# A hybrid decoder block in float32 on one core: the output projection takes one 2x2 block problem in column groups 1 and 2, and the turns come directly behind the settling

## What is computed

```
    x = x + 0.5 * swiglu(rms_norm(x, ffn1_norm[l]), ffn1_w_gate[l], ffn1_w_up[l], ffn1_w_down[l])
    ...
    x = x + jnp.concatenate([y_conv, y_attn], axis=-1) @ w_out[l]
    x = x + 0.5 * swiglu(rms_norm(x, ffn2_norm[l]), ffn2_w_gate[l], ffn2_w_up[l], ffn2_w_down[l])
```

## Time and profile before

| | us |
|---|---|
| median of 3 runs | 1764.33 (1763.83 to 1764.43) |
| profiled execution, its own time | 1764.07 |
| its span, first to last instruction | 1762.2 |
| PE busy | 1750.1 (99%) |
| DVE busy | 1508.9 (86%) |
| ACT busy | 1052.0 (60%) |
| output projection, four groups | 977.5 to 1065.5 |

### The profile page before, as it was taken

The page is one execution under the profiler, slowest core; times in us unless marked ns, Lnnn a source line. Parts: engine busy times, 40 slices in busy tenths (PEclk is TensorE's granted clock), DMA queues, the critical chain, the costliest instruction groups (busy, mean ns, idle before and its releaser), DMA issues.

```text
span 1762.2 us, 21424 instructions
## 1 busy us (share of the span) xinstructions
PE 1750.1 (99%) x7797; PEld 1440.9 (82%) x7797; DVE 1508.9 (86%) x1741; ACT 1052.0 (60%) x1258; POOL 303.7 (17%) x585
## 2 busy tenths in 40 slices
PE   9999999999999999999999999999999999999998
PEld 7888888888888888888888888888888888888886
DVE  7799999999887786777877768899999999887786
ACT  7566666666555554555555456566666666555544
POOL 0102211111112112111121141021111111210001
PEclk9999999999999999999999999999999999999999
DMA  7756666666676667657555577666666666676654
GB/s 266 239 197 219 206 213 222 227 221 212 207 238 215 216 194 235 203 172 222 192 179 173 194 227 254 220 209 205 217 222 229 225 216 216 208 254 205 220 188 132
DMA packets 201801, 374.91 MB, mean 213 GB/s; under 512 B 19808, under 2 KB 20448, under 8 KB 201696
## 3 DMA queue, kind: packets, MB, share of 16 engines
q1 hardware_dynamic: 182848, 351.84, 60.6%
q0 software_dynamic: 18272, 21.01, 4.1%
q10 hardware_dynamic: 576, 0.69, 0.1%
HBM read 351.44 MB, written 4.19 MB: 202 GB/s over the span
## 4 chain that ended last, share of the span: by engine, by line
PE 98%; DVE 1%; DMA 1%; ACT 0%; issue 0%; SPq 0%; DVEq 0%; ACTq 0%
PE bank L854 17%; PE bank L856 17%; PE bank L857 17%; PE bank L871 9%; PE bank L873 9%; PE bank L872 9%; PE bank L992 4%; PE bank L995 4%; PE bank L994 4%; PE bank L837 2%; PE bank L836 2%; PE bank L835 2%; DMA raw<-in_ffn_w_gate_dram 0%; PE bank L1154 0%; PE bank L1171 0%; DMA x<-in_x_dram 0%
## 5 line engine op out<-in xcount | busy, mean ns | idle before, releaser
L1688 DVE TENSOR_TENSOR w_lo<-raw,w_hi 128x1024 fp32r<-128x1024 f32 x447 | 545.8, 1225 | 146.6 <-ACT w_hi L1249 142.2
L1249 ACT ACTIVATE w_hi<-raw 128x1024 fp32r<-128x1024 f32 x447 | 471.6, 1058 | 318.8 <-PE bank L857 195.8
L2478 POOL DMA_DIRECT2D turn_in<-gate x448 | 219.0, 497 | 820.2 <-DVE gate L1788 744.7
L854 PE MATMUL bank<-w_hi,xT_hi 128*128 128x512 f32 x812 | 318.3, 392 | 0.4 <-DVE xT_lo L1781 0.3
L856 PE MATMUL bank<-w_lo,xT_hi 128*128 128x512 f32 x812 | 316.0, 389 | 0.0
L857 PE MATMUL bank<-w_hi,xT_lo 128*128 128x512 f32 x812 | 316.0, 389 | 0.0
L854 PE MATMUL bank<-w_hi,hT_hi 128*128 128x512 f32 x528 | 205.5, 389 | 0.7 <-DVE w_lo L1688 0.7
L856 PE MATMUL bank<-w_lo,hT_hi 128*128 128x512 f32 x528 | 205.4, 389 | 0.0
L857 PE MATMUL bank<-w_hi,hT_lo 128*128 128x512 f32 x528 | 205.4, 389 | 0.0
L1263 ACT ACTIVATE w_hi<-first_b 128x1024 fp32r<-128x1024 f32 x140 | 148.7, 1062 | 91.0 <-PE bank L857 38.4
L1263 ACT ACTIVATE w_hi<-second_b 128x1024 fp32r<-128x1024 f32 x129 | 136.9, 1062 | 104.8 <-DVE second_b L1955 47.4
(11 more groups left out here) (239 smaller groups left out, 2865.0 us busy)
## 6 DMA issues: line engine op xcount, KB each, us to landing
raw<-in_ffn_w_down_dram SPq DMA_DIRECT2D x132, 512.0 KB, 4.9
raw<-in_ffn_w_up_dram SPq DMA_DIRECT2D x102, 512.0 KB, 6.4
raw<-in_ffn_w_gate_dram SPq DMA_DIRECT2D x101, 512.0 KB, 5.7
raw<-in_w_in_dram SPq DMA_DIRECT2D x80, 512.0 KB, 4.2
first_b<-in_ffn_w_gate_dram SPq DMA_DIRECT2D x40, 512.0 KB, 4.5
first_b<-in_ffn_w_up_dram SPq DMA_DIRECT2D x40, 512.0 KB, 4.6
second_b<-in_ffn_w_gate_dram SPq DMA_DIRECT2D x34, 512.0 KB, 5.2
second_b<-in_ffn_w_up_dram SPq DMA_DIRECT2D x34, 512.0 KB, 5.4
```

The lines of the kernel that those rows point to most:

```text
L854: pe.matmul(acc, hi[:, kt, ts], w_hi[slot][:, kk], start=(opens and kk == 0), stop=False, skip_group_check=problems(ffn, c) > 0)
L1249: act.activation(w_hi[f % RING][:], raw[m % RING][:], ACT.Copy).then_inc(hi_ready, 1)
L1688: dve.tensor_tensor(w_lo[f % RING][:], src[:], w_hi[f % RING][:].bitcast(F32), ALU.subtract)\
L2478: pool.dma_start(to[32 * j:32 * j + 32, q].rearrange("r k t i -> r (k t i)"), mid[32 * q:32 * q + 32, j].rearrange("r k t i -> r (k t i)") ...
```

## The change

The output projection gets one block problem: the first two K-chunks in order (`order[0]`, `order[1]`: the token tiles 8 to 11) of column groups 1 and 2. The two groups keep 6 plain chunks each, and the seven products stand among those of group 1. P1 and P6, P7 go to bank 5, P5 and P3 to bank 4, P2 and P4 straight onto the banks of group 1. Since the partial sums belong to two groups, DVE adds them onto `x` in six operations (`out_add`), after P1, P5, P6, chunk 4, P7 and P2; P3 waits for the second of these adds, P7 for the third, and the settling of groups 1 and 2 for all six. The sums of weight blocks are four operations in `low_out`. The token sums are made in the mixer's last part: `out_tokens` at B, chunk 4, `token_sum` at C, chunk 3, and the split at X, chunk 3 (ACT) and 5 (DVE). The weight blocks are read into `kept_down` and the buffers of parts K and V, four loads in place of four chunk loads.

Besides, `turn_quads` stands directly behind the settling of its group, ahead of the next split, and `split_block` moves: for block 0 to P7 of group 1, for block 1 to k = 4 of the 6 chunks of group 2, for block 2 as before to k = 6 of group 3. ACT's squares of groups 0 and 1 write their unused output to banks 6 and 7.

```
+def out_unit(g):
+    if g == OUT_PAIR:
+        return (0, P1, 1, P5, 2, P3, 3, P6, 4, P7, P2, P4, 5)
+    return tuple(range(CD - out_skipped(g)))
...
+OUT_PAIR = 1
+OUT_FORMS = [(g, k) for g in range(XG) for k in out_unit(g)]
+OUT_BLOCKS_AT = {1: (OUT_PAIR, P7), 2: (2, 4), 3: (3, 6)}
...
             def project(base, w, order):
+                for g, k in OUT_FORMS:
+                    if k in CHAIN + (P2, P4):
+                        continue
+                    load(base + OUT_AT[g, k], w, order[out_skipped(g) + k], g * W)
+                    if (g, k) == (OUT_PAIR - 1, 4):
+                        sp.wait_ge(lo_ready, CH_MIX + MIX_AT[J - 1, V, P7] + 1)
+                        load_block(mix_b11, b11_loaded[0], left, order[0])
+                    if (g, k) == (OUT_PAIR - 1, 5):
+                        load_block(b12, b12_loaded[0], right, order[0])
+                    if (g, k) == (OUT_PAIR - 1, 6):
+                        load_block(b22, b22_loaded[0], right, order[1])
+                    if (g, k) == (OUT_PAIR + 1, 0):
+                        sp.wait_ge(summed[0], SUMS * OUT_GROUPS_BEFORE + 2)
+                        load_block(b12, b12_loaded[0], left, order[1])
...
+            def out_product(f, hi, lo, p):
...
+                if p == P1:
+                    product(f, 5, a_hi[0][0], a_lo[0][0], opens=True, seen=True, on_sums=False)
+                if p == P5:
+                    pe.wait_ge(token_lo[0], OUT_TOKENS + 1)
+                    product(f, 4, s_hi[1][1], s_lo[1][1], opens=True, seen=True, on_sums=False)
+                if p == P3:
+                    pe.wait_ge(out_added, 2)
+                    product(f, 4, s_hi[0][1], s_lo[0][1], seen=True)
+                if p == P6:
+                    product(f, 5, s_hi[0][0], s_lo[0][0], seen=True)
+                if p == P7:
+                    pe.wait_ge(out_added, 3)
+                    product(f, 5, s_hi[1][0], s_lo[1][0], seen=True)
+                if p == P2:
+                    product(f, mine, a_hi[0][1], a_lo[0][1])
+                if p == P4:
+                    product(f, mine + 1, a_hi[1][1], a_lo[1][1])
...
+            def project(pr, q, r, early):
+                for f, (g, k) in enumerate(OUT_FORMS):
+                    high_out(f + RING)
+                    if g == 0:
+                        early(k)
+                    if OUT_BLOCKS_AT.get(g) == (g, k):
+                        split_block(r, g - 1)
+                    if k == out_last(g):
+                        dump = 6 if g < 2 else 4
...
+                if u == X and k == 3 and j == J - 1:
+                    act.wait_ge(chunk_used, CH_MIX + MIX_AT[J - 1, V, P7] + 1)
+                    split_tokens(LAST, 0, OUT_TOKENS + 1)
...
+            def out_tokens():
+                tiles = slice(OUT_TILES, OUT_TILES + 2 * KC)
+                dve.wait_ge(chunk_used, CH_MIX + MIX_AT[J - 1, V, P7] + 1)
+                dve.wait_ge(turned_lo, TB_HEAD + HJ)
+                dve.tensor_tensor(first_s[:], yT_hi[:, tiles].bitcast(F32), yT_lo[:, tiles].bitcast(F32), ALU.add)\
+                   .then_inc(token_sums[0], 1)
...
+            def low_out(f):
...
+                if p == P1:
+                    dve.wait_ge(b11_loaded[0], 16 * (OUT_GROUPS_BEFORE + 1))
+                    dve.wait_ge(b12_loaded[0], 32 * OUT_GROUPS_BEFORE + 16)
+                    dve.tensor_tensor(b12[:], b12[:], mix_b11, ALU.subtract).then_inc(summed[0], 1)
+                if p == P3:
+                    dve.wait_ge(lo_ready, CH_OUT + f + 1)
+                    dve.wait_ge(summed[0], n + 1)
+                    dve.tensor_tensor(b22[:], b22[:], b12[:], ALU.subtract).then_inc(summed[0], 1)
+                if p == 3 and in_pair:
+                    dve.wait_ge(lo_ready, CH_OUT + OUT_AT[OUT_PAIR, P1] + 1)
+                    dve.wait_ge(summed[0], n + 2)
+                    dve.tensor_tensor(mix_b11, b22[:], mix_b11, ALU.subtract).then_inc(summed[0], 1)
+                if p == P2:
+                    dve.wait_ge(lo_ready, CH_OUT + f + 1)
+                    dve.tensor_tensor(b12[:], b12[:], b22[:], ALU.subtract).then_inc(summed[0], 1)
...
+            def out_add(i):
+                p, of, far, t = ((P1, 5, 0, 0), (P5, 4, 1, 1), (P6, 5, 1, 0), (P3, 4, 1, 0), (P7, 5, 0, 1), (P7, 5, 1, 1))[i]
+                dve.wait_ge(x_saved, 1 + XG)
+                dve.wait_ge(chunk_used, CH_OUT + OUT_AT[OUT_PAIR, p] + 1)
+                if i in (3, 5):
+                    dve.wait_ge(out_added, {3: 3, 5: 2}[i])
+                dve.tensor_tensor(x[:, t, cs], bank[of][:], x[:, t, cs], ALU.add).then_inc(out_added, 1)
...
+            def project(pr, q, r, early):
+                for f, (g, k) in enumerate(OUT_FORMS):
+                    if k == out_last(g):
+                        dve.wait_ge(squares_ready, q + g)
+                        dve.wait_ge(x_saved, r + g + 1)
+                        if g > 0:
+                            dve.wait_ge(turned_lo, TB_X2 + 2 * g)
+                        if g in (OUT_PAIR, OUT_PAIR + 1):
+                            dve.wait_ge(out_added, LATE_SUMS)
+                        for t in range(TT):
+                            unit_done(CH_OUT + f + 1, pr + g // 2, g % 2, t)
+                            dve.scalar_tensor_tensor(out=turn_in[:, t], in0=bank[2 * (g % 2) + t][:], scalar=1.0,
+                                                     in1=x[:, t, g * W:(g + 1) * W], op0=ALU.mult, op1=ALU.add)\
+                               .then_inc(drained[g % 2], 1)
+                        if g < XG - 1:
+                            dve.wait_ge(drained[g % 2], (pr + g // 2 + 1) * TT)
                             turn_quads(turn_in, block_turned)
...
+                    if g == OUT_PAIR:
+                        if k == P1:
+                            out_add(0)
+                        if k == P5:
+                            out_add(1)
+                        if k == P6:
+                            out_add(2)
+                        if k == 4:
+                            out_add(3)
+                        if k == P7:
+                            out_add(4)
+                        if k == P2:
+                            out_add(5)
+                    low_out(f + RING)
+                    if g == 0:
+                        early(k)
+                    if OUT_BLOCKS_AT.get(g) == (g, k):
+                        split_block(TB_X2, g - 1)
+                    if k == out_last(g) and g < XG - 1:
...
+                if j == J - 1:
+                    if u == B and k == 4:
+                        out_tokens()
+                    if u == C and k == 3:
+                        token_sum(LAST, 0, OUT_TOKENS)
+                    if u == X and k == 5:
+                        split_tokens(LAST, 0, OUT_TOKENS)
```

More of the change, by code:

```diff
@@ L180 @@
 CH_OUT = CH_MIX + MIX_FORMS
-CH_FFN2 = CH_OUT + XG * CD
+CH_FFN2 = CH_OUT + len(OUT_FORMS)
 CH_END = CH_FFN2 + FORMS[1]
@@ L223 @@
 MIX_TOKENS = late_token_use(0) + 1
+OUT_TOKENS = MIX_TOKENS + 1
+OUT_TILES = KC * OUT_ORDER[0]
 PR_FFN1 = 0
@@ L824, in _, with unit @@
         def _(pe):
-            def unit(base, second, hi, lo, chunks, k, order=None, tiles=range(TT)):
-                pe.wait_ge(lo_ready, base + k + 1)
-                slot = (base + k) % RING
-                tile = order[k] if order else k
-                for t in tiles:
+            def unit(f, second, hi, lo, tile, opens, ends):
+                pe.wait_ge(lo_ready, f + 1)
+                slot = f % RING
+                for t in range(TT):
                     acc = bank[2 * second + t][:]
@@ new lines, in project @@
+            def project(ch, pr, hi, lo, ready, order, early):
+                for g, k in OUT_FORMS:
+                    f = ch + OUT_AT[g, k]
+                    if k in CHAIN + (P2, P4):
+                        out_product(f, hi, lo, k)
+                        continue
+                    if k == 0:
+                        banks_free(pr + g // 2, g % 2)
+                    if g == 0:
+                        ready(k)
+                    unit(f, g % 2, hi, lo, order[out_skipped(g) + k], opens=(k == 0), ends=(k == out_last(g)))
+                    if k == 0 and g == 0:
+                        early()
```

102 lines of the change are left out of this document (48 added, 54 removed).

## The result

| | before | after |
|---|---|---|
| median of 17 runs each, same chip | 1764.11 us | 1768.41 us |
| lowest to highest | 1763.83 to 1764.48 | 1765.65 to 1770.12 |
| profiled execution, its own time | 1764.07 | 1768.5 |

The change makes the kernel slower by 4.3 us. The ratio of the times is 1.0022, 95% interval 1.0015 to 1.0029, so the loss is real, and its size lies across the 0.2% (3.5 us) that the prediction took as its bound. The time is inside the predicted range and 1.8 above the predicted number. It is 0.5 above the interval of A, the favoured theory (1764.3 to 1767.9), and so lies in the part of the range that was C's, with a chance of 0.24. One thing in the table was not foreseen at all: the runs of after spread over 4.5 us, those of before over 0.65.

The account below looks back on a forecast made before the run. PE was taken to bound the kernel. Terms -1.36 (matmuls), +0.4 (head 1), +0.9 (pair) and +2.4 (group 3) sum to +2.3 us on 1764.07, giving 1766.4, as median 1766.6; range 1762.9 to 1768.8.

Parts of the forecast that it names:

- A: Favoured: the saving is less than DVE and the block's return cost, net 0 to +3.5 us (1764.3 to 1767.9); chance 0.54.
- C: Block 1 returns at least 1.2 us later, PE waits 3.6 or more at group 3, over 0.2% slower (1768.1); chance 0.24.
- 6 matmuls fewer: Output projection: 48 matmuls become 42, at 0.227 us each, taking at most 1.36 us off PE.
- head 1: Mixer's softmax: `first_s` ahead of the settling delays DVE's factors for this head, so PE loses 0.4 us.
- the pair: Projection group 1: PE waits for DVE's adds onto `x`, 0.5 us at P3 and 0.4 at P7, 0.9 together.
- group 3, fourth chunk: Projection: PE waits 2.4 us for this chunk's `w_lo`, queued on DVE behind the late return of block 1.
- What bounds the kernel: Whole kernel: PE sets the time, busy 1750.1 of 1762.2 us, so removed matmuls count in full unless something comes late.
- Token sums: Mixer, among the softmax heads: `first_s` delays head 1's factors, 0.4 us lost; the other pieces cost nothing.
- The settling of group 1: DVE in the projection: it ends 5.0 us behind PE's start of group 2, where before it was some 3.4.
- The move of block 1: Projection: first DMA 1.6 us behind the settling, transfer 13.2, chunk ready 7.1 after landing; 2.4 lost at group 3.
- B: The waits don't appear and the saving arrives, net -1.4 to 0 us, 1763.0 if whole; chance 0.20.
- If ACT's wait is under 3 us, the size at group 3 is wrong: Sign in the next profile: ACT's wait ahead of block 1's split, forecast 5 us, tests the 2.4 at group 3.

Follow-up runs that it names:

- experiment 9: Changed kernel with block 1's DMAs shared by GpSimd and ACT, first token sum two chunks earlier, third weight sum behind second add onto `x`: 1763.01 us, ratio 0.9995.

## Why the prediction was right, and what it missed

In us, on the profiled executions; "measured" from the starts of PE's matmuls in after:

| term | forecast | measured |
|---|---|---|
| 6 matmuls fewer | -1.36 | -1.36 |
| head 1 | +0.4 | +0.3 (0.48 between starts for 0.23, and 0.07 for a slower first matmul behind it) |
| the pair, P3 and P7 | +0.9 | +0.97 (0.34 and 0.41, and 0.11 for a slower first matmul behind each) |
| group 3, fourth chunk | +2.4 | +3.1 (3.0, and 0.11 behind it) |
| half clock behind it | not in the sum | +1.6 |
| sum | +2.3 | +4.6 |

1764.07 + 4.6 = 1768.7 for the 1768.5 of the profiled execution, so the table leaves nothing of the loss to be found elsewhere. The kernels with eight DMAs and with shared DMAs bear out its upper half: -1.36 + 0.3 + 0.97 = -0.1, and they gave 1763.95 and 1764.03 beside 1764.25 and 1763.92.

The time fell into the range, but partly by luck. The range's upper end, 1768.8, was made of a later landing (C) and of a pair that costs 2; neither came as large, and the half clock, which no term stood for, took up that room. The end is also mis-added: a pair at 2 instead of 0.9 adds 1.1 and not 0.7, which gives 1769.2.

- **What bounds the kernel**: held. Each loss is a place where PE waits for DVE, and DVE's total (1522 us) never mattered.
- **Token sums**: right in place and cause; 0.1 too much. Moving `first_s` took the gap away (experiment 9).
- **The pair**: right, within 0.1. The order of two operations on DVE is worth a third of a microsecond at P3, as experiment 9 shows.
- **The settling of group 1** "5.0 us behind PE's start of group 2": 4.4 by the profile.
- **The move of block 1**: the mechanism was right and the size short. "I take 13.2" was 13.9; the row of this very block, 14.09, was the nearer one, and its gap of 1.5 in the issues is back in after (1.51 ahead of the sixteenth DMA), and in every other profile in which POOL issues all 16 for block 1. It belongs to this place, and I had discounted it as an accident of one execution. Why it stands there is not known; in after the moves of the other two blocks have none. The chain behind the landing was 7.4 for 7.1 (0.55 for 0.21 ahead of the settling). Together the wait was 3.0 for 2.4.
- **The missed step**: the sum priced a wait of PE at its own length. Behind this one the granted clock fell to 1.2 GHz in two of three profiled executions, 1.6 us more in the first profile. Without it the forecast is close: the third profile of the changed kernel had no such stretch and took 1766.41, for a forecast of 1766.4. That it is this close is luck. The measured terms without the clock add up to +3.0 and not +2.3, and this execution ran on a chip where before took 1763.88, and with a wait 0.2 shorter.
- **Rivals**: C's mechanism (the return of block 1, price one for one with its landing) is also A's, and is the one seen, at a loss of 3.0 and not C's 3.6; the clock's part carried the time past the bound that divided the two. C's outcome came, by a cause that was not C's. B's condition never came near: ACT waited for the block 3.67 us, after the 2.70 and 1.85 for chunk loads that I had not foreseen and that hid some of the 5 us. "If ACT's wait is under 3 us, the size at group 3 is wrong" was a poor sign for that reason; the landing time is the thing to read. The 0.24 for "slower" was too little for a place whose price has only one sign.

## What to carry to other kernels

When a change shortens the stage behind which a transfer hides, follow the transfer's landing, not the engines' busy times: here two chunks less in group 2 took 5.4 us of cover from a return that had 1.9 to spare, and the return is mostly a queue of issues, which a second issuer shortened by 3.8 us. A wait of the engine that sets the time may cost more than its length; if the profile shows PE's starts at twice their usual distance behind a wait, add that stretch, and expect the runs to spread. Take more than one profile then: one execution with the stretch, or one without it, says little about the median. A block problem that saves 6 matmuls has 1.36 us to give, and three waits of a third of a microsecond for adds and sums use up nearly all of it; only the order of single operations on DVE wins it back.

## What the runs showed of the hardware that was not expected

- Around PE waits of 2.7 to 4.1 us the granted clock fell to 0.50 in five profiled executions and stayed at 1.00 in two, the longest wait without a fall being 3.7; at the one of 1.5 it stayed at 1.00. Two falls came inside the wait, 0.9 and 1.2 us before its end, one at its end, and two when PE had been at work again for 0.8 and 1.4 us.
- The half clock lasted 3.4 us in three of them and 6.8 us in the two that began inside the wait. It cost 1.6 us where all 3.4 fell on matmuls, and 2.8 to 2.9 in the two long ones.
- The first matmul behind even a short wait is slower: 0.33 to 0.34 to the next start instead of 0.227, at P3, P7 and group 3 alike, at full clock.
- An extra split of 128x1024 on DVE took 1.22 us, and 1.94 where POOL's copy stood beside it.
- ACT issues one of these DMAs in 0.64 us, GpSimd in 0.49.
